# Seven block products in place of eight in the first feed-forward product of a decoder trunk

## The reference, cut to what matters

```python
h = rms_norm(x, norm_ffn_pre[i])                      # 512 x 1024
gate, up = split_cols(h @ w_ffn_in[i], (D_FF, D_FF))  # 1024 x 5632
f = (jax.nn.silu(gate) * up) @ w_ffn_out[i]           # 2816 x 1024
x = x + rms_norm(f, norm_ffn_post[i])
```

## Time and profile before

| | us |
|---|---|
| median of 3 runs | 1282.7 (1282.38 to 1282.84) |
| the profiled execution | 1282.91 |
| its span | 1280.9 |
| TensorE (PE) busy | 1268.3 |
| DVE, ACT, POOL busy | 560.4, 444.5, 130.0 |
| strips 3 to 21 of the first product, each layer | 206.8, 203.1 of records |

### The profile page before, as it was taken

The page is one execution under the profiler, slowest core; times in us unless marked ns, Lnnn a source line. Parts: engine busy times, 40 slices in busy tenths (PEclk is TensorE's granted clock), DMA queues, the critical chain, the costliest instruction groups (busy, mean ns, idle before and its releaser), DMA issues.

```text
span 1280.9 us, 16193 instructions
## 1 busy us (share of the span) xinstructions
PE 1268.3 (99%) x6677; PEld 1096.4 (86%) x6677; DVE 560.4 (44%) x841; ACT 444.5 (35%) x764; POOL 130.0 (10%) x225
## 2 busy tenths in 40 slices
PE   9999999999999999999999999999999999999998
PEld 8999987988888888887899989889888888888876
DVE  5674636433333332237466646464333333222463
ACT  6443425222222221125455444253222222211351
POOL 2003612000000000001120038030000000000010
PEclk9999999999999999999999999999999999999999
DMA  7222132433333232323231223224333332223111
GB/s 250 92 80 70 66 99 67 133 113 99 99 99 99 96 98 90 128 82 95 67 98 55 87 83 100 83 69 132 93 94 94 92 97 99 99 99 132 66 50 66
DMA packets 124184, 122.03 MB, mean 95 GB/s; under 512 B 5200, under 2 KB 109008, under 8 KB 124112
## 3 DMA queue, kind: packets, MB, share of 16 engines
q1 hardware_dynamic: 124112, 121.01, 30.7%
HBM read 118.90 MB, written 2.10 MB: 94 GB/s over the span
## 4 chain that ended last, share of the span: by engine, by line
PE 80%; DVE 2%; ACT 1%; issue 1%; POOL 1%; ACTq 0%; DVEq 0%; POOLq 0%
PE bank L659 25%; PE bank L661 25%; PE bank L660 25%; PE bank L793 1%; DVE upd L1395 1%; PE bank L842 0%; PE bank L865 0%; PE bank L911 0%; POOL tiny L1203 0%; ACT junk L1036 0%; PE bank L863 0%; DVE x L1402 0%; ACT junk L1038 0%; ACT junk L1004 0%; PE bank L895 0%
## 5 line engine op out<-in xcount | busy, mean ns | idle before, releaser
L1304 DVE TENSOR_TENSOR w_lo<-raw,w_hi 128x1024 fp32r<-128x1024 f32 x162 | 192.1, 1226 | 457.4 <-ACT w_hi L977 457.4
L977 ACT ACTIVATE w_hi<-raw 128x1024 fp32r<-128x1024 f32 x162 | 162.9, 1052 | 452.5 <-PE bank L661 452.5
L659 PE MATMUL bank<-h_hi,w_hi 128*128 128x512 f32 (+1 forms) x800 | 291.3, 364 | 2.0 <-DVE h_lo L1368 2.0
L660 PE MATMUL bank<-h_lo,w_hi 128*128 128x512 f32 (+1 forms) x800 | 290.9, 364 | 0.0
L661 PE MATMUL bank<-h_hi,w_lo 128*128 128x512 f32 (+1 forms) x800 | 290.8, 364 | 0.0
L659 PE MATMUL bank<-w_hi,h_hi 128*128 128x384 f32 (+2 forms) x576 | 206.7, 359 | 1.7 <-DVE ple_n L1395 1.0
L661 PE MATMUL bank<-w_hi,h_lo 128*128 128x384 f32 (+2 forms) x576 | 200.4, 348 | 0.0
L660 PE MATMUL bank<-w_lo,h_hi 128*128 128x384 f32 (+2 forms) x576 | 200.2, 348 | 0.0
L659 PEld LDWEIGHTS bank<-h_hi,w_hi 128*128 128x128 f32 x800 | 151.0, 189 | 26.4 <-issue 2.8
L661 PEld LDWEIGHTS bank<-h_hi,w_lo 128*128 128x128 f32 x800 | 151.0, 189 | 23.8
L660 PEld LDWEIGHTS bank<-h_lo,w_hi 128*128 128x128 f32 x800 | 151.0, 189 | 23.5
(11 more groups left out here) (170 smaller groups left out, 1284.0 us busy)
## 6 DMA issues: line engine op xcount, KB each, us to landing
raw<-in_w_ffn_in SPq DMA_DIRECT2D x88, 512.0 KB, 4.7
raw<-in_w_ffn_out SPq DMA_DIRECT2D x44, 512.0 KB, 4.2
raw<-in_w_in SPq DMA_DIRECT2D x40, 384.0 KB, 3.9
raw<-in_w_out SPq DMA_DIRECT2D x16, 512.0 KB, 4.1
raw<-in_w_gate SPq DMA_DIRECT2D x16, 512.0 KB, 4.0
raw<-in_w_in SPq DMA_DIRECT2D x10, 512.0 KB, 4.2
raw<-in_w_ple SPq DMA_DIRECT2D x4, 512.0 KB, 5.2
x<-in_x_in SPq DMA_DIRECT2D x3, 512.0 KB, 7.3
```

The lines of the kernel that those rows point to most:

```text
L659: pe.matmul(out_ap, a_hi, b_hi, start=start, stop=False, skip_group_check=True)
L660: pe.matmul(out_ap, a_hi, b_lo, start=False, stop=False, skip_group_check=True)
L977: last = act.activation(w_hi[g % SLOTS][:, j * n + cols.start:j * n + cols.stop], raw[q % RAWS][:, cols], ACT.Copy, scale=1.0 if col is No ...
L1304: last = dve.tensor_tensor(lo, raw[q % RAWS][:, cols], hi, ALU.subtract)
```

## The change

Strips 0 to 2 (PLAIN) stay as they are. In strips 3 to 21 (FAST) the product of a strip is seen as 2 x 2 blocks: the weight as A11, A12 (gate, rows 0 to 511 and 512 to 1023), A21, A22 (up), and h transposed as four blocks by k half and by row half. It is made by Strassen's scheme in Winograd's form: seven products P1 to P7 of 4 k x 3 matmuls of 256 columns. This needs

- once a layer: four combinations T1 to T4 of the blocks of h (`differences`, from a copy `h_raw` of the first two tiles and from the transposes' banks), and their splits T_hi, T_lo (event `Tc`);
- per strip, of weights: S1 = A21 + A22, S2 = S1 - A11, S4 = A12 - S2, S3 = A11 - A21 on DVE (`combo`, line 1697), then splits of A11 and A12 together (`hi_gate`, `lo_gate`), of A22 (`hi_up`, `lo_up`) and of the four combinations (`hi_combo`, `lo_combo`);
- per strip, of results: ACT copies P1, P5 and one sum out of PSUM (`one`, `five`, `two`), DVE adds them back (`v` line 1792, `c12` line 1807, `c22` line 1733); P2 adds into P1's bank, P3 into P5's, and P7 and P4 into P6's. silu and the product with up are made in halves of 256 (`mid1`, `mid2`).

P7 and P4 of a strip are issued one step later, among the products of the next strip. The middle values are kept unsplit in `mid` and are split by events `split` in the last steps and in the second product. f[2]'s `w_lo` moves behind tile 3's `pre` on DVE. The load of post_ffn's weights moves from strip 6 to `fo` 3. Three operand sets more (`ext_*`, `w_sum`) and other addresses go with it.

```diff
+def slot_of(g):
+
+    layer, s = divmod(g, NS)
+    return (layer * (NS - NF + 1) + (s if s < FO0 else s - NF + 1)) % SLOTS
...
+def plan_products():
+
+    order = []
+    for j in FAST:
+        order += [(1, j), (5, j), (6, j)]
+        order += [(7, j - 1)] if j > PLAIN else []
+        order += [(3, j), (2, j)]
+        order += [(4, j - 1)] if j > PLAIN else []
+    return order + [(7, LAST), (4, LAST)]
+
+
+PRODUCTS = plan_products()
+OPERANDS = ["A11", "A12", "S1", "S3", "A22", "S2", "S4"]
+LEFT = {1: "A11", 2: "A12", 3: "S4", 4: "A22", 5: "S1", 6: "S2", 7: "S3"}
+RIGHT = {1: (0, 0), 2: (1, 0), 3: (1, 1)}
+USED_BY = {left: p for p, left in LEFT.items()}
+COMBOS = ["S1", "S2", "S4", "S3"]
+LOWS = ["A11", "S1", "S2", "S4"]
...
+        add("hraw", 1)
         add("post", "mix", 3)
-        close(o[3])
+        add("hi", SIDX[f[2]])
         mm(f[0], 0)
         add("T", "ffn", 2)
+        add("diff", 0, 0)
         add("pre", "ffn", 3)
+        add("lo", SIDX[f[2]])
+        add("diff", 0, 1)
         mm(f[1], 0)
         add("T", "ffn", 3)
+        add("diff", 1, 0)
+        add("diff", 1, 1)
         mm(f[2], 0)
-        for j in range(3):
-            mm(f[j], 1)
-            close(f[j])
-            add("mid", j)
-        for j in range(3, FCH):
-            mm(f[j], None)
-            close(f[j])
-            add("mid", j)
-        for s in fo[:-2]:
+        mm(f[0], 1)
+        add("Tc")
+        add("mid", 0)
+        add("first")
+        mm(f[1], 1)
+        add("mid", 1)
+        mm(f[2], 1)
+        add("mid", 2)
+        for j in FAST:
+            add("step", j)
+            if LAST - 5 <= j < LAST - 1:
+                add("split", j - LAST + 5)
+        add("last7")
+        mm(fo[0], 3)
+        add("last4")
+        add("conv", SIDX[fo[1]])
+        add("split", 4)
+        add("split", 5)
+        for m in (0, 1, 2):
+            mm(fo[0], m)
+        add("conv", SIDX[fo[2]])
+        close(fo[0])
+        add("split", 6)
+        add("split", 7)
...
+            for k in (2 * i + 6, 2 * i + 7):
+                if k < FCH:
+                    add("split", k)
...
+            def product(layer, p, j):
+
+                n = nth(layer, j)
+                g = layer * NS + F0 + j
+                if p == 1:
+                    if j >= PLAIN + 2:
+                        pe.wait_ge(st_silu1, n - 2)
+                    else:
+                        pe.wait_ge(prod_ready, layer * PLAIN + 1)
+                elif p == 5:
+                    if j >= PLAIN + 2:
+                        pe.wait_ge(st_silu2, n - 2)
+                    else:
+                        pe.wait_ge(prod_ready, layer * PLAIN + 2)
+                elif p == 6:
+                    if j >= PLAIN + 2:
+                        pe.wait_ge(st_mid1, n - 2)
+                    else:
+                        pe.wait_ge(prod_ready, layer * PLAIN + 3)
+                elif p == 3:
+                    pe.wait_ge(st_five, n)
+                elif p == 2:
+                    pe.wait_ge(st_one, n)
+                elif p == 7:
+                    pe.wait_ge(st_c12, n)
+                else:
+                    pe.wait_ge(st_c22, n)
+                if p == 7:
+                    pe.wait_ge(lo_ready, 2 * g + 1)
+                elif p == 4:
+                    pe.wait_ge(lo_ready, 2 * g + 2)
+                elif p != 2:
+                    pe.wait_ge(st_lo, 4 * (n - 1) + LOWS.index(LEFT[p]) + 1)
+                if p >= 4 and j == PLAIN:
+                    pe.wait_ge(t_lo, 4 * layer + 4)
+                hi, lo, _ = operand(layer, LEFT[p], j)
+                for k in range(4):
+                    if p < 4:
+                        a, b = RIGHT[p]
+                        cols = slice(b * S // 2, (b + 1) * S // 2)
+                        r_hi, r_lo = h_hi[:, 4 * a + k, cols], h_lo[:, 4 * a + k, cols]
+                    else:
+                        i = {5: 0, 6: 1, 7: 2, 4: 3}[p]
+                        r_hi, r_lo = T_hi[:, i, k, :], T_lo[:, i, k, :]
+                    c = slice(k * P, (k + 1) * P)
+                    last = mm3(st_bank(p, j)[:, 0:256], hi[:, c], lo[:, c], r_hi, r_lo,
+                               k == 0 and p in (1, 5, 6), k == 3)
+                last.then_inc(st_mm, 1)
...
+                elif kind == "hraw":
+                    m = e[1]
+                    for half in range(2):
+                        act.wait_ge(h_lo_ready, t_count(layer, "ffn", m, half))
+                        act.activation(h_raw[:, half, :, m * P:(m + 1) * P],
+                                       banks[2 * m + half][:, :].rearrange("p (k t) -> p k t", k=4),
+                                       ACT.Copy).then_inc(h_raw_ready, 1)
+                elif kind == "Tc":
+                    for i in range(4):
+                        act.wait_ge(t_raw, 8 * layer + 5 + i)
...
+                elif kind == "step":
+                    j = e[1]
+                    n = nth(layer, j)
+                    if j < LAST:
+                        hi_gate(layer, j + 1)
+                        hi_combo(layer, "S1", j + 1)
+                    hi_up(layer, j)
+                    if j < LAST:
+                        hi_combo(layer, "S2", j + 1)
+                    act.wait_ge(st_mm, st_count(layer, 1, j))
+                    if j > PLAIN:
+                        act.wait_ge(st_v, n - 1)
+                    act.activation(one[:], st_bank(1, j)[:, 0:256], ACT.Copy).then_inc(st_one, 1)
+                    act.wait_ge(st_mm, st_count(layer, 5, j))
+                    if j >= PLAIN + 2:
+                        act.wait_ge(st_mid2, n - 2)
+                    act.activation(five[j % 2][:], st_bank(5, j)[:, 0:256], ACT.Copy).then_inc(st_five, 1)
+                    if j < LAST:
+                        hi_combo(layer, "S4", j + 1)
+                    act.wait_ge(st_v, n)
+                    if j > PLAIN:
+                        act.wait_ge(st_c12, n - 1)
+                    act.activation(two[:], st_bank(6, j)[:, 0:256], ACT.Copy).then_inc(st_two, 1)
+                    if j < LAST:
+                        hi_combo(layer, "S3", j + 1)
+                    else:
+                        conv(layer * NS + FO0, (0,))
+                    act.wait_ge(st_c12, n)
+                    if j > PLAIN:
+                        act.wait_ge(st_mid2, n - 1)
+                    act.activation(silu_u[:], st_bank(3, j)[:, 0:256], ACT.Silu).then_inc(st_silu2, 1)
+                    if j == LAST:
+                        conv(layer * NS + FO0, (1,))
+                    act.wait_ge(st_mm, st_count(layer, 2, j))
+                    if j >= PLAIN + 2:
+                        act.wait_ge(st_mid1, n - 2)
+                    else:
+                        act.wait_ge(prod_ready, (layer + 1) * PLAIN)
+                    act.activation(silu_g[:, j % 2 * 256:j % 2 * 256 + 256], st_bank(2, j)[:, 0:256],
+                                   ACT.Silu).then_inc(st_silu1, 1)
+                elif kind == "split":
+                    k = e[1]
+                    if k < PLAIN:
+                        act.wait_ge(prod_ready, layer * PLAIN + k + 1)
+                    else:
+                        act.wait_ge(st_mid1, nth(layer, k))
+                        act.wait_ge(st_mid2, nth(layer, k))
+                    act.wait_ge(*mid_free(layer, k))
+                    act.activation(mid_hi(k), mid[:, k, :].rearrange("p (h t) -> p h t", h=2),
+                                   ACT.Copy).then_inc(mid_hi_ready, 1)
...
+            def differences(layer, p, part):
+
+                cols = slice(p * P, (p + 1) * P)
+                top, low = (banks[4 + 2 * p + i][:, :].rearrange("p (k t) -> p k t", k=4) for i in range(2))
+                t1, t2, t3, t4 = (T_sum[:, i, :, cols] for i in range(4))
+                if part:
+                    landed(combos["T2"])
+                    done(dve.tensor_tensor(t3, t2, h_raw[:, 0, :, cols], ALU.subtract), t_raw)
+                    done(dve.tensor_tensor(t4, h_raw[:, 1, :, cols], t2, ALU.subtract), t_raw)
+                    return
+                dve.wait_ge(h_raw_ready, 4 * layer + 2 * p + 2)
+                landed(done(dve.tensor_tensor(t1, top, h_raw[:, 0, :, cols], ALU.subtract), t_raw))
+                combos["T2"] = done(dve.tensor_tensor(t2, low, t1, ALU.subtract), t_raw)
...
+                elif kind == "step":
+                    j = e[1]
+                    c = j + 1
+                    more = c <= LAST
+                    if more:
+                        combo(layer, "S1", c)
+                    if j >= PLAIN + 2:
+                        mid1(layer, j - 2)
+                    if more:
+                        combo(layer, "S2", c)
+                        lo_gate(layer, c)
+                        combo(layer, "S4", c)
+                    lo_up(layer, j)
+                    if more:
+                        lo_combo(layer, "S1", c)
```

(58 more changed lines are left out.)

244 lines of the change are left out of this document (201 added, 43 removed).

## The result

The changed kernel takes 1253.99 us (median of 4 runs, 1253.44 to 1254.62), the kernel before 1282.72 in the same comparison: a ratio of 0.9777, 95% interval 0.976 to 0.9794, faster by 28.7 us. The forecast was 1253.7.

The account below looks back on a forecast made before the run. The prediction took TensorE's own work to bound the kernel, busy 1268.3 of 1280.9 us. Its terms, -30.4 + 1.2 + 0.2 = -29.0, took the profiled 1282.9 to 1253.9 us, median 1253.7; range 1250 to 1267.

Parts of the forecast that it names:

- TensorE's work: Strips 3 to 21: 84 matmuls of 256 columns take 10.08 us per strip for 10.88; -30.4 us over 38 strips.
- No wait in the steps: Strassen steps: DVE and ACT keep up, operands are there in time, so TensorE never waits; 0 us.
- The walk for the even step: One Strassen step followed through DVE, ACT and TensorE: c22 tightest with 1.5 us to spare, DVE idle 0.8 until P4.
- One of the prediction's signs: In the changed profile, DVE 85 to 95% busy in strips 3 to 21.
- The front: Before the Strassen strips: f[2]'s first block starts 0.6 us later per layer, +1.2 us in both layers.
- Behind the strips: After step 21: conv(fo[0]), DVE's last work there, ends about when P7(21) does; +0.1 us per layer, +0.2.
- Every product restarts TensorE: Strassen strips: each product's first matmul takes 0.20 us, not 0.12; 21 us more, 1275 us; chance 0.05.
- The gap is shorter with products: Strassen strips: half the fixed 0.0133 us per matmul vanishes, 9.5 us per strip; -52 us, 1232 us; chance 0.03.
- DVE becomes the bound, and slower than before: Strassen steps: DVE's round of 15 operations takes 11.03 us, over the old 10.88; 36 us more, 1290 us; chance 0.05.
- DVE's operations would cost more for their two or three waits: Strassen steps: 0.05 to 0.1 us more per DVE operation, round 10.4 us; 13 us more, 1267 us; chance 0.10.

Follow-up runs that it names:

- halves: The kernel before with strips 3 to 21 in two halves of 256 columns each, no Strassen: 1307.01 us.
- w_lo_back: The changed kernel with strip 2's w_lo split back in its old place on DVE, ahead of tile 2's h_lo: 1255.98 us.
- the kernel with four additions: The changed kernel with four needless DVE additions of 448 elements between S3 and c22 in every Strassen step but the last: 1311.02 us.

## Why the prediction was right

- **TensorE's work, -30.4 us.** The products take 191.71 us per layer for 191.5 forecast; the saving is 15.0 per layer, 30.0. The 0.120 and 0.2267 us of the kernel before held with other operands and other banks, and *halves* shows the split into columns and a fixed part apart from Strassen. The gap of N / 2.4 + 2.5 ns that the Trainium skill gives (TensorE: Matmul & The Clock Gate, Back-to-back issue gap) would have made it 45, an estimate. The same section calls this the gap of an isolated matmul, which the prediction does not say. The starts here are 0.120 and 0.2267 us apart, each matmul with a weight load of its own, and not 0.109 and 0.216.
- **No wait in the steps.** Right but for 0.2 us per layer at the start of P3 of strip 3. The walk for the even step was close. DVE's and ACT's timelines of the changed kernel, the step whose P1 starts at 334.47 (256.51 + 7.4 + 7 x 10.08):

```profile
334.67 0.42 DVE L1726 TENSOR_TENSOR mid<-silu_g,bank 128x256 f32<-128x256 f32 x1 [0.83 <-PE bank L801]
...
338.99 0.43 DVE L1792 TENSOR_TENSOR bank<-bank,one 128x256 f32<-128x256 f32 x1 [0.35 <-PE bank L801]
...
340.43 0.69 DVE L1697 TENSOR_TENSOR w_sum<-raw,raw 128x512 f32<-128x512 f32 x1 [0.41 <-PE bank L801]
341.04 0.42 DVE L1733 TENSOR_TENSOR five<-bank,five 128x256 f32<-128x256 f32 x1
...
337.55 0.38 ACT L1289 ACTIVATE five<-bank 128x256 f32<-128x256 f32 x1 [0.91 <-PE bank L801]
```

 Mid1 starts 0.20 into the step, v 4.52, S3 5.96, c22 ends at 7.0; the walk had 0.2, 4.5, 6.0 and 7.0, and the idle 0.8 before mid1. The copy of P5 ends at 3.5, as walked. The durations guessed for 256 elements, 0.42 and 0.37, came out at 0.42 to 0.43 and 0.37 to 0.38. ACT's splits of 512 elements, 0.60 in the prediction, take 0.62 to 0.63, which costs nothing here. One of the prediction's signs is just missed: from 264 to 446 us DVE is busy 151.91 of 182.00 us, 83%, where 85 to 95% was given; its own figure of 8.5 us in 10.08 makes 84%.
- **The step it missed.** It checked v and c22 of strip 3's step and not the copy of P5, which in the first step has S2's split in front of it and no P7 between P6 and P3. 0.4 us in all. (A slip without effect: it counts eight more differences behind f[2]'s `w_lo`, and there are six, since the two before it are of the same eight.)
- **The front, +1.2.** 0.6 per layer, as taken. Its two parts held in the main: the two copies ahead of tile 3's squares cost next to nothing, since POOL's next step was held up by DVE's split in any case, and POOL's step for xn was not held up by h_lo and the differences. POOL and DVE in the changed kernel:

```profile
223.33 0.60 POOL L1498 TENSOR_SCALAR tiny<-tiny 128x1 f32<-128x1 f32 x1 [3.16 <-ACT junk L1336]
...
228.61 0.22 POOL L1477 TENSOR_SCALAR tiny<-tiny 128x1 f32<-128x1 f32 x1 [4.03 <-ACT junk L1212]
...
221.41 2.35 DVE L1599 TENSOR_TENSOR w_lo<-raw,w_hi 128x1024 fp32r<-128x1024 f32 x2
...
227.25 1.28 DVE L1663 TENSOR_TENSOR h_lo<-bank,h_hi 128x512 fp32r<-128x512 f32 x2
228.45 0.68 DVE L1678 TENSOR_TENSOR T_sum<-bank,h_raw 128x512 f32<-128x512 f32 x1
```

 The first starts 0.9 later than in the earlier trace rows and ends at nearly the same time, 223.93 for 223.95, right behind w_lo. Counted from strip 0's first block it ends 4.60 us in, and 4.47 before: about 0.1 of the copies' 1.1 us did get through. From the end of x of tile 3 (227.34) to the block it is 6.04 us, and the prediction had 6.14 (227.36 to 233.5). So the 0.6 rests on two offsets of 0.1 that cancel. The second took 1.08 beside w_lo and takes 0.22 beside the first difference (L1678), which has one input in PSUM and one in SBUF; in *w_lo_back* it stands beside w_lo again and takes 1.08 again. That is what the Trainium skill says of the port pair (SBUF — State Buffer, SBUF: two separate sides): a DVE operation with two SBUF inputs holds it for its whole length, and here one with a single SBUF input doesn't.
- **Behind the strips, +0.2.** There is no wait: 446.67 to 446.79 is an even 0.12. The second piece of w_lo was ready in time. So two small errors of opposite sign stood in the sum, 0.4 and -0.2 us. The span came out at 1252.1 for 1280.9 - 29.0 = 1251.9. That the medians agree to 0.3 us is in part luck: the runs of the changed kernel lie 1.2 us apart, and the profiled one, 1254.62, is 0.7 over the 1253.9 forecast for it.
- **The rivals.** *Every product restarts TensorE* and *The gap is shorter with products* are out: the starts are 0.12 apart over 19 strips, but for strip 3's P3. *DVE becomes the bound, and slower than before* did not happen, and it takes some 2.5 us more per round to get there. With them the round is 11.09 us, as that rival had it (11.03), but the kernel takes 1311 us and not 1290: the ends of the stretch and the clock add what the even rounds don't, and the round closes through P7 and P4 and not by DVE's queue alone. That DVE's operations would cost more for their two or three waits is out for the even steps; they overlap by the same 0.07. Only where an operation waits for the result of the one just before it does it start later, about 0.1 us behind that one's end (S2 behind S1 in the first step, 258.73 for an end at 258.63).

## What to carry to other kernels

Fewer multiplications pay only what is left after the fixed cost per matmul: measure the two shapes' time from start to start first, and divide. When work moves to an engine that is then over 80% busy, its share says little; walk one round of its queue against the bound engine's needs, and then the first and the last rounds separately, since that is where the room is used up. A block that waits for all pieces of an operand may be able to begin with the first; here that was worth 1.35 us.

## What I had not expected

In the kernel with four additions TensorE's granted clock falls inside the Strassen stretch. Its rows by stretch (us, then busy time of PE, PEld, DVE, ACT, POOL, granted clock, DMA):

```profile
277.10:280.30 3.20, 3.20 (x17) 3.20 (x16) 2.98 (x8) 2.41 (x5) 0.00 (x0) 0.50 0.17 48
...
289.30:300.00 10.70, 10.24 (x84) 10.04 (x84) 10.32 (x19) 5.40 (x11) 0.00 (x0) 1.00 0.33 98
```

0.50 is the lower of its two levels, 1.2 GHz. Before it fell TensorE had stood for 1.34 and then 2.44 us; sixteen matmuls there are 0.214 apart for 0.120, 1.5 us lost. The same happens twice more in the layer, after the first and the third of the three waits of 1.74 us near the splits. The waits of 0.76 us in every even step never bring it about, nor does the second wait of 1.74, and in the changed kernel the granted clock is 1.00 over the whole stretch of the products. What decides between these cases was not tried. A late operand can cost more than its own wait: here 9 of 57 us.
